# Expert weights loaded as halves of the contraction instead of gate and up matrices

## The reference

```python
scores = jax.nn.sigmoid(ht @ w_router)                    # (256, 64)
# the 8 best experts of the 4 best groups of each token, their scores normalised: combine (256, 64)
a = jnp.einsum('td,edf->tef', hb, w_gate)                 # w_gate, w_up: (64, 1024, 256)
u = jnp.einsum('td,edf->tef', hb, w_up)
return jnp.einsum('tef,efd->td', jax.nn.silu(a) * u * cb[..., None], w_down)   # w_down: (64, 256, 1024)
```

## Time and profile before

| what | value |
|---|---|
| median of three runs | 1598.61 us |
| the profiled execution, its own time | 1598.61 us |
| its span | 1596.7 us |
| PE (TensorE matmul) busy | 1518.0 us, 95% |
| DVE (VectorE) busy | 950.7 us, 60% |
| ACT (ScalarE) busy | 763.3 us, 48% |
| POOL (GpSimd) busy | 116.9 us, 7% |
| moved by DMA | 360.12 MB, 226 GB/s over the span |
| 4 chain by line, largest | DMA proj<-in_w_exp_up 9%; PE psum L3074 7% |

### The profile page before, as it was taken

How to read it: one execution, slowest core, us unless ns; L and a number is a source line. 1 busy time by engine, 2 the same in 40 slices (tenths; PEclk the granted TensorE clock), 3 DMA queues, 4 the chain that set the end, 5 groups by cost and what they waited for, 6 DMA issues and landing times. The chain is left out here.

```text
span 1596.7 us, 37817 instructions
## 1 busy us (share of the span) xinstructions
PE 1518.0 (95%) x15431; PEld 1227.5 (77%) x15431; DVE 950.7 (60%) x1366; ACT 763.3 (48%) x971; POOL 116.9 (7%) x66
## 2 busy tenths in 40 slices
PE   7998899999999999999999999989999999999996
PEld 6997877899999989999887888866555555555553
DVE  3496434267664467754300524576888687878875
ACT  4446216344333468532113225334667666667673
POOL 0321400002331000001200000000000000000000
PEclk9999999999999999999999999989999999999998
DMA  8557356545554545552122233438999899999993
GB/s 269 176 176 227 122 164 221 202 158 185 183 182 180 168 132 159 159 159 80 56 80 80 80 106 110 140 153 336 413 407 399 360 409 409 416 416 385 414 405 144
DMA packets 178015, 360.12 MB, mean 226 GB/s; under 512 B 9165, under 2 KB 137658, under 8 KB 161338
## 3 DMA queue, kind: packets, MB, share of 16 engines
q1 hardware_dynamic: 177850, 357.81, 61.5%
HBM read 355.03 MB, written 1.05 MB: 223 GB/s over the span
## 5 line engine op out<-in xcount | busy, mean ns | idle before, releaser
L350 PE MATMUL psum<-proj_r 128*128 128x256 f32 x1392 | 344.2, 287 | 3.9 <-ACT proj_r L314 3.9
L351 PE MATMUL psum<-proj_r 128*128 128x256 f32 x1392 | 341.7, 285 | 0.0
L319 DVE TENSOR_TENSOR ring_r<-ring,proj_r 128x2048 fp32r<-128x2048 f32 x94 | 226.4, 2409 | 159.1 <-ACT proj_r L314 158.5
L2361 DVE COPY ring<-proj 128x1024 f32 x378 | 239.4, 687 | 96.0 <-POOLq L1376 59.7
L350 PEld LDWEIGHTS psum<-proj_r 128*128 128x128 f32 x1392 | 270.7, 194 | 7.2 <-issue 6.2
L351 PEld LDWEIGHTS psum<-proj_r 128*128 128x128 f32 x1392 | 270.4, 194 | 0.1
L314 ACT ACTIVATE proj_r<-ring 128x2048 fp32r<-128x2048 f32 x93 | 177.5, 1909 | 106.5 <-PE psum L354 94.1
L1771 ACT ACTIVATE ring<-proj 128x1024 f32 x186 | 188.9, 1051 | 7.7 <-issue 5.9
L354 PE MATMUL psum<-proj_r,ring_r 128*128 128x256 f32 x1392 | 182.0, 284 | 2.6 <-DVE ring_r L319 2.6
L354 PEld LDWEIGHTS psum<-proj_r,ring_r 128*128 128x128 f32 x1392 | 173.9, 193 | 3.0 <-DVE ring_r L319 2.8
L453 PE MATMUL psum<-u,ring 128*128 128x256 f32 x512 | 121.7, 386 | 1.2 <-ACT proj L1604 1.1
(11 more groups left out here) (529 smaller groups left out, 2390.1 us busy)
## 6 DMA issues: line engine op xcount, KB each, us to landing
ring<-in_w_in SPq DMA_DIRECT2D x65, 1024.0 KB, 5.2
proj<-in_w_exp_gate SPq DMA_DIRECT2D x64, 1024.0 KB, 9.7
proj<-in_w_exp_up SPq DMA_DIRECT2D x64, 1024.0 KB, 10.3
proj<-in_w_exp_down SPq DMA_DIRECT2D x64, 1024.0 KB, 8.4
ring<-in_w_ada SPq DMA_DIRECT2D x24, 1024.0 KB, 7.8
ring<-in_w_ffn_in SPq DMA_DIRECT2D x22, 1024.0 KB, 5.1
ring<-in_w_ffn_out SPq DMA_DIRECT2D x11, 1024.0 KB, 4.9
ring<-in_w_out SPq DMA_DIRECT2D x8, 1024.0 KB, 5.0
```

Of the source, the lines that this page charges most:

```text
L319: dve.tensor_tensor(ring_r[:, at.slot, :], ring[:, at.slot, :], self.heads[at.buffer].bitcast(F32), ALU.subtract) \
L350: pe.matmul(dst, w, xh, start=start, stop=False, skip_group_check=True)
L351: pe.matmul(dst, w, xl, start=False, stop=False, skip_group_check=True)
L2361: ins = dve.tensor_copy(into_copy[k_half][j][:, kind * D:(kind + 1) * D], pieces[:, bass.ds((piece + kind) & 7, 1), of_half].rearrange("p ...
```

## The change

A place of the ring holds other bytes. The first two pieces of an expert are no longer its gate and its up matrix, but the two halves of the contraction: piece 0 holds half 0 of the gate weights (4 KB on each partition) and behind it half 0 of the up weights, piece 1 the same of half 1. The down piece holds what it held. Each piece is now loaded by two DMAs of 512 KB, both on the piece's semaphore, for which POOL now waits until 32. For the down piece these two DMAs read rows 0 to 127 and 128 to 255 of the matrix.

`copy_into` becomes one copy of 128 x 2048, since what goes into a copy buffer now stands in one piece in the same order.

SP's wait changes with it: for a place whose predecessor held piece 0 or 1, it waits for `into_copied` at `ended * 2 + kind_before`, where `kind_before` is 0 or 1.

```diff
             sp.wait_ge(over, 4 * 8)
+            half_d = KD // 2 * DE
             for at, e, kind in piece_order:
...
                     if kind_before < 2:
-                        sp.wait_ge(*reached("into_copied", ended * 2 + (ended & 1)))
+                        sp.wait_ge(*reached("into_copied", ended * 2 + kind_before))
                     else:
                         sp.wait_ge(*reached("down_copied", ended))
                 dst = pieces[:, (at + 1) % 8, :]
-                if kind < 2:
-                    src = fp[("w_exp_gate_2", "w_exp_up_2")[kind]][0, e].rearrange("(p k) n -> p (k n)", p=P)
-                else:
-                    src = fp["w_exp_down_2"][0, e].rearrange("(f p) n -> p f n", p=P)
-                    dst = dst.rearrange("p (f n) -> p f n", f=2)
-                sp.dma_start(dst, src).then_inc(sig(f"piece_loaded_{at % 8}"), 16)
+                for part in range(2):
+                    if kind < 2:
+                        src = fp[("w_exp_gate_2", "w_exp_up_2")[part]][0, e].rearrange("(p k) n -> p (k n)", p=P)[:, kind * half_d:(kind + 1) * half_d]
+                    else:
+                        src = fp["w_exp_down_2"][0, e, part * P:(part + 1) * P, :]
+                    sp.dma_start(dst[:, part * 1024:(part + 1) * 1024], src).then_inc(sig(f"piece_loaded_{at % 8}"), 16)
...
-                pool.wait_ge(*reached(f"piece_loaded_{at % 8}", 16 * loads_before[at % 8]))
+                pool.wait_ge(*reached(f"piece_loaded_{at % 8}", 32 * loads_before[at % 8]))
...
-                of_half = slice(k_half * D, (k_half + 1) * D)
-                for kind in range(2):
-                    ins = dve.tensor_copy(into_copy[k_half][j][:, kind * D:(kind + 1) * D],
-                                          pieces[:, bass.ds((piece + kind) & 7, 1), of_half].rearrange("p o n -> p (o n)"))
-                ins.then_inc(sig("into_copied"), 1)
+                dve.tensor_copy(into_copy[k_half][j], pieces[:, bass.ds((piece + k_half) & 7, 1), :].rearrange("p o n -> p (o n)"))                    .then_inc(sig("into_copied"), 1)
```

## The result

The changed kernel takes 1607.66 us (median of 4 runs, 1605.26 to 1613.85), the kernel before 1599.06 us (4 runs). The ratio is 1.0053, with a 95% interval of 1.0035 to 1.0073: 5.6 to 11.7 us slower. The forecast was 1603.6, with a range of 1596 to 1611.

The account below looks back on a forecast made before the run. The prediction took the expert stage's weight transfers as the bound, TensorE close behind. Packets +5.9, early release -1.4, late release +0.7 and copies -0.2 made +5.0 us on 1598.61: 1603.6 us, range 1596 to 1611.

Parts of the forecast that it names:

- likeliest case: Whole kernel: the forecast itself, +2.5 to +7.5 us, or 1601.1 to 1606.1 us; chance 0.46.
- shallow ring: Expert stage: late release leaves fewer pieces in flight through even ends, +5.6 us, 1609 us; chance 0.11.
- packets: Expert stream: gate and up rows cut from 8 KB to 4 KB cost 0.11 us for 54 experts, +5.9 us.
- release behind four blocks: After the expert with four blocks: piece 0 is freed one copy earlier, so the next load leaves sooner, -1.4 us.
- What bounds: Expert stage: transfers bound at 7.75 us per expert, TensorE close behind at 7.61.
- The late release at the start: Start of the expert stage: at even ends piece 1 waits for the next pair's first copy, +0.7 us.
- SyncE's second DMA: Each piece's load: 0.33 us more on SP, delaying a piece's end at most that much after an idle queue.
- Copies: Behind a few landings: one 128 x 2048 copy replaces two of 128 x 1024, -0.2 us in all.
- A cost of microseconds for every further DMA: All 192 pieces: the skill's 2.0 us fixed cost per DMA paid in full, some hundreds of microseconds; chance 0.01.

Follow-up runs that it names:

- e7: The changed kernel with the old count for freeing places, both pieces free when half 1 of the expert's last block is copied: 1607.24 us, ratio 1.0057.
- e8: The kernel before, with each gate or up piece loaded by one DMA in 4 KB rows from two halves of the matrix: 1603.44 us, ratio 1.0036.
- e4: The kernel before, with the down piece also read in 8 KB rows and gate and up columns taken in steps of two: 1598.53 us, ratio 0.9998.
- e1: The kernel before, its copies and release kept, with each piece loaded by two DMAs in 4 KB rows: 1608.84 us, ratio 1.0055.
- e6: The changed kernel with SP waiting for exactly the copy that frees each place, a repeat beside the changed kernel on one chip: 1599.45 us, ratio 1.0002.
- e5: The changed kernel as it is, run again beside three others on one chip: 1608.07 us, ratio 1.0060 against the kernel before.

## Why the prediction came out as it did

The direction, the mechanism and the range held; the size was 5.0 us against 8.6. 1607.66 lies outside the likeliest case's own band (1601.1 to 1606.1) and near the 1609 of the shallow ring, which is not what happened. The 8.4 us between the two traces divide like this:

| stretch | forecast | found |
|---|---|---|
| T to the landing of expert 7 | +0.7 | +1.8 |
| expert 7 to 63 (packets +5.9, release behind four blocks -1.4) | +4.5 | +5.6 |
| behind the landing of expert 63 | -0.2 | +1.0 |

Point by point, from T in the two traces:

**What bounds.** Right. The last up piece landed 494.5 us after T before and 501.9 after; in the changed kernel the chain reads

```profile
1243.28 9.15 DMA proj<-in_w_exp_up
```

and

```profile
1557.75 9.87 DMA proj<-in_w_exp_up
```

so from 1252.43 to 1567.62 40 experts took 315.19 us, 7.88 each, at the edge of the 7.83 to 7.88 that the forecast named.

**Packets: mis-sized.** 0.11 us per expert was forecast, near the low end of 0.07 to 0.30. The steady stream gives 7.67 against 7.53 between landings, and over the ten experts 36 to 46 7.82 against 7.67: 0.14 to 0.15. The pure stretches of the earlier trace rows had only one size, and the term for the end packets was guessed. From expert 23 to 63 the forecast was 40 x 0.11 = 4.4; it was 5.4 (315.2 against 309.8). Ahead of expert 20 it was too large: from expert 7 to 20 the traces differ by -0.1 us, where 1.4 were forecast. There the landings of the kernel before have longer gaps of their own (8.8 us at expert 15, 9.0 at expert 20). So the price per expert was too low and the number of experts that pay it too high, and the two errors cancel in part by luck.

**The late release at the start: mis-sized, +0.7 forecast, about 2 us found.** Expert 7 landed 57.2 us after T against 55.4. The place: SyncE's load after the copy of the next pair, SyncE first, then the copies (two in one row, the first over at 1097.64):

```profile
1089.23 1.01 SPq L1307 DMA_DIRECT2D proj<-in_w_exp_down  x2
1097.67 0.33 SPq L1307 DMA_DIRECT2D proj<-in_w_exp_gate  x1
...
1099.07 0.33 SPq L1307 DMA_DIRECT2D proj<-in_w_exp_gate  x1
```

```profile
1096.41 2.36 DVE L2360 COPY ring<-proj 128x2048 f32 x2 [7.21 <-PE psum L3071]
```

7.21 us of idle VectorE stand before that copy, and SyncE idle with it. Of the 2.5 us of transfer lost, less came back than assumed. e7, which has the old wait and the same packets, was level with the kernel before at expert 7 (55.7 against 55.4), so 1.5 to 1.7 us of the loss here is the release.

**The early release behind four blocks: right as a release, not as a gain.** SyncE and VectorE there:

```profile
1239.67 0.81 SPq L1307 DMA_DIRECT2D proj<-in_w_exp_down  x2
1241.48 0.34 SPq L1307 DMA_DIRECT2D proj<-in_w_exp_gate  x1
...
1242.91 0.33 SPq L1307 DMA_DIRECT2D proj<-in_w_exp_gate  x1
1243.28 1.18 SPq L1307 DMA_DIRECT2D proj<-in_w_exp_up  x1
```

```profile
1237.28 2.36 DVE L2360 COPY ring<-proj 128x2048 f32 x2 [2.02 <-PE psum L3071]
...
1239.76 1.22 DVE L2360 COPY ring<-proj 128x2048 f32 x1
```

The load left at 1239.67, right behind the copy for (half 0, j 1); (half 1, j 0) ended at 1240.98, 1.3 us later. e7, without it, took 29.1 us from expert 20 to 23, the changed kernel 27.8: 1.3 us won, as forecast. But the kernel before took 27.5. With six DMAs in the place of three, the last one left 3.6 us after the first instead of 2.1, and the queue was empty, so nothing hid it. The forecast had put SyncE's second DMA at 0.33 us. That this spread is what took the 1.3 us back is argued, not shown, and e8 speaks against it: with the old wait and one DMA per piece it took 29.0 us here, as much as e7 with two.

**Copies and the tail.** -0.2 was forecast; from the last up piece to the end it was +1.0. The tails in this order, the changed kernel and the kernel before (PE clock third from the end):

```profile
1567.00:1601.00 34.00, 19.65 (x143) 9.22 (x139) 13.39 (x14) 10.15 (x14) 2.34 (x1) 0.83 0.19 75
```

```profile
1564.00:1597.00 33.00, 19.95 (x167) 9.66 (x155) 14.36 (x19) 11.29 (x15) 2.34 (x1) 0.85 0.21 82
```

The granted clock was 0.83 against 0.85 there, which may be a part of that. The trace of the kernel before is the short one: its tail is 32.1 us, and every other kernel's of the table has 33.1 to 35.1, with e4's, where all packets are of 8 KB and the copies are the old ones, at 33.3. So the 1.0 us is hardly the change's. e7 and e1 differ in the copies and in where half of the bytes lie, and gave 1.0057 and 1.0055: 252 copies saved are worth nothing that these intervals can tell, as forecast.

**The rivals.** A cost of microseconds for every further DMA is out: one DMA or two per piece, the landings are 7.67 us apart. The shallow ring (+5.6) did not happen in the steady stretch: 77.9 to 78.5 us in every kernel with all packets of 4 KB, whatever its releases. But the rival was the nearer to the truth in one thing the forecast left out: releases matter, and in more places than the two it named. The forecast compared the new counts with the old ones, and never with the exact ones. The new count waits at an odd end for the next expert's first copy, and at an even end for the next pair's; with both exact the layout of the change costs nothing that the ratio shows, 1.0002.

**What stays open.** The medians put the exact releases 8.6 us under the changed kernel, the traces 4.3 (the means of two, 531.2 against 535.5 from T). Against the kernel before, the ratio of the exact releases is 1.0002, but their traces are 4.2 and 5.0 us longer from T. A part of both gaps goes with the granted clock. Its mean over the executions was 0.9824 in e6, 0.9797 in e5 and 0.9804 in the kernel before beside them. Among executions of one kernel, an execution with a clock lower by 0.001 took 1.1 us more (a straight line through all executions of the kernels in the table, each kernel about its own mean; in e6 alone it is nearly flat). By that estimate some 3 of the 8.6 us are clock, and at one clock the exact kernel would be about 2 us slower than the kernel before, not level with it. Whether the releases caused the difference in clock or it was chance is not shown. Nor is it settled whether a second DMA per piece costs where the queue has run empty.

## What to carry to other kernels

When a stream of loads is the bound, price its packets in the steady state, from the distance between landings of long stretches with nothing else waiting, and compare every byte's row length with the one it had. When pieces are cut so that they come free at different times, write down for each the very event that frees it and wait for that; a count that is one too high may wait for the next piece to land. In one queue look at an early release together with its neighbours': here each exact wait alone did less than both. And compare the granted clocks before a difference of a few microseconds is laid to an edit.

## What was not expected of the hardware

- A DMA onto 64 partitions with rows of 8 KB: two of them in the place of one onto 128 moved 205 GB/s at a busy share of 94%, where the whole ones moved 416. The Trainium skill (DMA: Bandwidth & Descriptors, Rules for kernel authors) says of two transfers to disjoint partition halves that they serialise, because both use the same 16 engines. That agrees with no gain from the split; how far the rate falls is what this run adds.
- Matmuls that read their moving columns in steps of two took 388 instead of 380 ns (e4).
